# Head mean squares from two rounded products, logarithm and exponential from one activation table, gates from the hyperbolic tangent

## The chip, the core and the metric

The kernel runs on one core of a Trainium2 chip. Its time is the device time of one launch in microseconds (us), from the first to the last instruction of the program and what the launch adds around them. Times of kernels are medians of several launches; everything else is read from one profiled execution.

The core has engines that each work through a list of instructions of their own, in order, and meet only through semaphores: PE (TensorE, matrix products; its output goes to PSUM), DVE (VectorE), ACT (ScalarE, activation functions out of tables), POOL (GpSimd, here used only to start DMAs) and SP (SyncE, used only to start DMAs).

## The reference

One layer of a decoder is computed for 1024 prompt tokens and 32 sample tokens (8 sequences of 4), so for T = 1056 columns. What matters for the change:

```python
z = rms_norm(x) @ w_in       # q (12 heads of 64) | k | v | ua | ub | ga | gb
q = rms_norm(q, q_norm_w)    # over each head's 64 values
k = rms_norm(k, k_norm_w)
u = ua * sigmoid(ub)
# three groups of 4 heads: dilated window attention, merged by their denominators
a  = o_att @ w_att
cb = silu(layer_norm(causal_dwconv(u))) @ w_conv_out
h  = sigmoid(ga) * a + sigmoid(gb) * cb
x  = x + h @ w_out
x  = x + (silu(g) * up) @ w_down
```

All inputs are float32. The head norm needs, for each head and token, the mean of 64 squares; with channels on partitions that is a product with a 128 by 128 matrix which holds 1/64 where row and column belong to one head.

## The kernel before, in words

Activations lie with channels on the 128 partitions and tokens in the free dimension, cut into NCH = 3 chunks of CH = 352 columns. A weight tile of 128 output channels is a job: its 8 input blocks of 128 channels times 3 chunks. Every large product is computed in three passes of a rounded format (fp32r): weights and activations are each split in a rounded part and the remainder (`whi`, `wlo`, `xhi`, `xlo`), and hi times hi, hi times lo and lo times hi are added up in PSUM (lines 675 to 677). So one chunk of a job is 24 matmuls. ACT makes the rounded weights `whi` (lines 1134, 1197), DVE the remainder `wlo` (line 1422), two jobs ahead.

The order of all work is written out by hand. The stages are:

1. GLU jobs (16), with a loop over 8 pairs. DVE multiplies value and sigmoid and then does 13 taps of the depthwise convolution per pair (lines 1465, 1466).
2. q, k, v jobs: 3 groups of 6 jobs, two each for q, k and v. In a job i of q or k (i < 4), ACT squares each chunk into `sqb` (line 1191). While PE is in the next job, it multiplies after each chunk the squares of the job before with `headmean`, a plain float32 product (line 763, function `mean_squares`). ACT takes the logarithm (line 1186) and the exponential with factor -0.5 (line 1188), which gives the reciprocal root in `rsb`. DVE then multiplies the product in PSUM with the norm's weight and `rsb` into `zt` (line 1517, `qkv_out`) or copies v (line 1519), and does 1, 2 and 2 taps of the convolution after the three chunks; every third job it also does the convolution of the sample tokens (lines 1498 to 1502).
3. The gate stage: 48 slots q, in each of which PE does one chunk of a gate job (`dense`), ACT the sigmoid of it (`gate`, line 1210), and around that one block of the window attention proceeds in steps: scores on PE (line 860), mask and maximum on DVE (line 1558), exponentials on ACT (line 1240), turning on PE (line 876), copies on DVE and ACT, and the product with the values on PE (line 889). The first slots also hold the rest of the convolution's taps, slots 25 to 28 the LayerNorm with its logarithms and exponentials (lines 1271, 1273), and slots 31 on the products of cached keys on DVE (line 1588), each of which needs a DMA of queries (`qb`) that POOL starts when the product two before it is done. Slots 41 to 44 hold swish (`ln_act`, line 1278).
4. 24 slots of the convolution's output projection, which start when DVE has made the first remainder `slo` (line 1667, `conv_lo`). DVE multiplies with the stored gate (`conv_gate`, line 1663).
5. The att stage: 24 units of 6 matmuls each. DVE multiplies the product in PSUM with the gate (line 1739), adds the convolution branch (line 1741), ACT rounds the sum to `hhi` (line 1359) and DVE makes the remainder `hlo` (line 1748). Then w_out and the norm.
6. The feed-forward part with the other weights, from 1097 us to the end.

The gates are stored to DRAM by SP as they are made and loaded again for stages 4 and 5.

The tables of ACT hold one set of functions at a time; the build puts an `ACT_TABLE_LOAD` wherever a function needs another set.

## Time and profile before

| | |
|---|---|
| time before, median of 3 runs | 1867.81 us (1867.55 to 1868.34) |
| the profiled execution's own time | 1867.85 us |
| its span, first to last instruction | 1866.0 us |
| busy: PE, DVE, ACT, POOL | 1784.8, 1028.7, 623.3, 69.8 us |
| instructions of PE, DVE, ACT | 10441, 1443, 1029 |
| mean granted clock of PE | 0.971 |

Busy time is the time in which an engine has at least one instruction under way. A timeline row has the start and the duration in us, the engine, the line and the operation, output and inputs, how many neighbouring instructions it merges, and in brackets how long the engine was idle before it and who ended that. PE's matmuls overlap: their starts, not their durations, tell how fast they follow each other. A row of a view by line has the count, the busy time, the mean duration in ns, and the idle time before the group with what ended it.

### The profile page before, as it was taken

The page shows a single profiled execution, that of the slowest core. Times are in us where ns is not written, and L with a number is a line of the kernel's source. Part 1 is how long each engine was busy: PE and PEld are TensorE (multiplying, and loading weights), DVE is VectorE, ACT ScalarE, POOL GpSimd, SP SyncE. Part 2 cuts the span into 40 slices and gives each one's busy share as a digit, 9 for nine tenths or more (in the row PEclk, how much of TensorE's full clock was granted, in tenths as well). Part 3 has the DMA queues.
Part 4 walks back from the last instruction along what each step waited for, and adds up shares of the span by engine and source line. Part 5 has one row for each costly group of instructions (what it writes and reads, how often), then busy time and mean ns, then how long its engine had stood idle before and what let it go on. Part 6 is the DMA issues. An engine that isn't in the chain of part 4 may idle for free.

```text
span 1866.0 us, 25465 instructions
## 1 busy us (share of the span) xinstructions
PE 1784.8 (96%) x10441; PEld 1670.0 (89%) x10441; DVE 1028.7 (55%) x1443; ACT 623.3 (33%) x1029; POOL 69.8 (4%) x125
## 2 busy tenths in 40 slices
PE   5999989999999997779999999999999999999999
PEld 5899989999888887779998889899899899899897
DVE  5688988788987355673175432424424424424425
ACT  5111165957666566810032232121121121121120
POOL 0000000000000001212000000000000000000000
PEclk8999999999999998988699999999999999999999
DMA  6111333234242326975382002222222222222232
GB/s 190 57 56 56 112 102 115 91 114 150 91 145 85 138 86 191 332 261 165 103 288 91 1 34 91 91 91 91 91 91 91 91 91 90 92 90 90 92 109 103
DMA packets 156487, 211.55 MB, mean 113 GB/s; under 512 B 9090, under 2 KB 127010, under 8 KB 155603
## 3 DMA queue, kind: packets, MB, share of 16 engines
q1 hardware_dynamic: 145971, 134.01, 23.4%
q0 software_dynamic: 10416, 76.16, 10.9%
q8 instruction: 68, 1.11, 0.2%
q14 instruction: 32, 0.26, 0.0%
HBM read 180.04 MB, written 74.80 MB: 137 GB/s over the span
## 4 chain that ended last, share of the span: by engine, by line
PE 85%; DVE 5%; DMA 3%; ACT 2%; SPq 2%; DVEq 2%; issue 1%; ACTq 0%
PE ps L675 19%; PE ps L676 19%; PE ps L677 19%; PE ps L1110 4%; PE ps L1108 4%; PE ps L1109 4%; DVE conv L1466 2%; PE ps L942 2%; PE ps L1038 2%; PE ps L1040 2%; PE ps L1039 2%; DMA qb<-scr_q 1%; PE ps L889 1%; DMA raw<-w_in 1%; SPq L471 1%
## 5 line engine op out<-in xcount | busy, mean ns | idle before, releaser
L675 PE MATMUL ps<-xhi,whi 128*128 128x352 f32 x1200 | 405.4, 338 | 8.6 <-DVEq L1521 7.0
L677 PE MATMUL ps<-xhi,wlo 128*128 128x352 f32 x1200 | 388.4, 324 | 0.0
L676 PE MATMUL ps<-xlo,whi 128*128 128x352 f32 x1200 | 387.9, 323 | 0.0
L675 PE MATMUL ps<-nhi,whi 128*128 128x352 f32 x1056 | 341.7, 324 | 0.0
L676 PE MATMUL ps<-nlo,whi 128*128 128x352 f32 x1056 | 339.4, 321 | 0.0
L677 PE MATMUL ps<-nhi,wlo 128*128 128x352 f32 x1056 | 338.9, 321 | 0.0
L1466 DVE SCALAR_TENSOR_TENSOR conv<-u,vec,conv 128x1024 f32<-128x1024 f32 x240 | 308.4, 1285 | 25.6 <-issue 11.1
L1422 DVE TENSOR_TENSOR wlo<-raw,whi 128x1024 fp32r<-128x1024 f32 x126 | 153.6, 1220 | 262.0 <-ACT whi L1197 253.6
L675 PEld LDWEIGHTS ps<-xhi,whi 128*128 128x128 f32 x1200 | 228.2, 190 | 19.1 <-DVEq L1521 7.6
L676 PEld LDWEIGHTS ps<-xlo,whi 128*128 128x128 f32 x1200 | 228.5, 190 | 4.1
L677 PEld LDWEIGHTS ps<-xhi,wlo 128*128 128x128 f32 x1200 | 227.9, 190 | 0.0
L675 PEld LDWEIGHTS ps<-nhi,whi 128*128 128x128 f32 x1056 | 198.9, 188 | 1.1
L676 PEld LDWEIGHTS ps<-nlo,whi 128*128 128x128 f32 x1056 | 199.1, 189 | 0.4
L677 PEld LDWEIGHTS ps<-nhi,wlo 128*128 128x128 f32 x1056 | 198.6, 188 | 0.0
L1197 ACT CAST whi<-raw 128x1024 fp32r<-128x1024 f32 x90 | 93.9, 1044 | 277.3 <-PE ps L1103 209.2
L1829 DVE TENSOR_TENSOR x<-x,ps 128x512 f32<-128x512 f32 x176 | 118.2, 686 | 78.8 <-PE ps L1110 78.4
L1110 PE MATMUL ps<-whi,aclo 128*128 128x512 f32 x352 | 138.8, 394 | 0.0
L1108 PE MATMUL ps<-whi,achi 128*128 128x512 f32 x352 | 138.8, 394 | 0.0
L1109 PE MATMUL ps<-wlo,achi 128*128 128x512 f32 x352 | 138.2, 393 | 0.0
L1816 DVE TENSOR_TENSOR sil<-ps,sil 128x352 f32<-128x352 f32 x66 | 34.6, 525 | 124.3 <-PE ps L677 124.3
L1398 ACT ACTIVATE sil<-ps 128x352 f32<-128x352 f32 x66 | 30.7, 465 | 190.4 <-PE ps L677 190.4
L675 PE MATMUL ps<-shi,whi 128*128 128x352 f32 x192 | 69.1, 360 | 22.7 <-DVE slo L1667 21.8
(208 smaller groups left out, 2262.6 us busy)
## 6 DMA issues: line engine op xcount, KB each, us to landing
kv_sample<-cache_kv_w POOLq DMA_DIRECT2D x32, 1022.0 KB, 6.2
raw<-w_in SPq DMA_DIRECT2D x50, 512.0 KB, 4.7
raw<-w_gate_up SPq DMA_DIRECT2D x44, 512.0 KB, 3.9
scr_z<-zt SPq DMA_DIRECT2D x34, 528.0 KB, 3.2
kc<-cache_kv_w POOLq DMA_DIRECT2D x32, 512.0 KB, 6.1
qb<-scr_q POOLq DMA_DIRECT2D x24, 512.0 KB, 6.3
raw<-w_down SPq DMA_DIRECT2D x22, 512.0 KB, 4.1
kv_sample<-cache_kv_w POOLq DMA_DIRECT2D x8, 1016.0 KB, 6.6
```

What stands on the lines that cost most here:

```text
L675: pe_mm(out, wh, rhs_hi, start=first, stop=False)
L676: pe_mm(out, wh, rhs_lo, start=False, stop=False)
L677: return pe_mm(out, wl, rhs_hi, start=False, stop=last)
L942: mm = nc.tensor.matmul(ps[:, 3, hp * P + col:hp * P + col + w], kc[m % 3][:, s if g else DEC_S - 1, hp * P:(hp + 1) * P], ptr[:, g, 0, co ...
L1038: nc.tensor.matmul(dst, hhi[:, k, tok], wohi[half][:, k, :], start=k == 0, stop=False)
L1108: nc.tensor.matmul(dst, achi[i % 2][:, k, tok], whi[half][:, cc], start=k == 0, stop=False)
L1109: nc.tensor.matmul(dst, achi[i % 2][:, k, tok], wlo[half][:, cc], start=False, stop=False)
L1110: mm = nc.tensor.matmul(dst, aclo[i % 2][:, k, tok], whi[half][:, cc], start=False, stop=k == 1)
L1197: act.copy(whi[n % 2][:, :], raw[n % 2][:, :]).then_inc(s_hi, 1)
L1422: V.tensor_tensor(wlo[slot][:, :], raw[slot][:, :], whi[slot][:, :].bitcast(F32), ALU.subtract).then_inc(s_lo, 1)
L1466: return V.scalar_tensor_tensor(dst, src, w, dst, ALU.mult, ALU.add)
L1829: last = V.tensor_tensor(x1_half(t, half), x1_half(t, half), ps[0:n, d % RING, :], ALU.add)
```

## The change

The change has three parts.

- **Mean squares.** ACT squares each chunk of q and k twice, once into `sqb` in float32 and once into a rounded tile `sqh`; DVE subtracts the two into a rounded remainder `sql` (new function `square_lo`), as its first work in each chunk's step; PE multiplies both with a rounded copy `headmean_r` (made once by DVE) and adds them up in PSUM. PE now waits for `sql`.
- **Tables.** ACT loads ahead of the q, k, v jobs a set of tables that holds both logarithm and exponential.
- **Gates.** The stored gate is tanh(z/2) in place of sigmoid(z) = (1 + tanh(z/2))/2. The "+ 1" goes into the multiplications with the gates (`conv_gate`, `att_gate`), which become operations with two arithmetic steps, and the factor 0.5 into the rounding of the sum (`att_hi`, `att_lo`).

```diff
--- before.py
+++ after.py
@@ -184,6 +184,10 @@
     pb = reg("pb", [P, NH, 2 * P])
     kvv = reg("kvv", [P, KT, GW])
     assert cur2[0] <= nc.sbuf_usable_end
+    sqh = at("sqh", [P, T], F32R, U0 + KT * ULEN * 4 + 2048)
+    sql = at("sql", [P, T], F32R, U0 + KT * ULEN * 4 + 2048 + T * 4)
+    headmean_r = at("headmean_r", [P, P], F32R, U0 + KT * ULEN * 4 + 2048 + 2 * T * 4)
+    assert KT * HIST * 4 + KT * NS * 4 <= 2048 and U0 + KT * ULEN * 4 + 2048 + 2 * T * 4 + 4 * P <= nc.sbuf_usable_end
     rowqk = at("rowqk", [P, NG, 2, HD], F32, U0 + KT * ULEN * 4 + 3 * GW * 4)
     cur2 = [cur2[0] - KT * GW * 4]
     prow = reg("prow", [P, NG, 2 * P])
@@ -239,7 +243,7 @@
     s_g, s_gfd, s_a, s_af = (sem(n) for n in ("s_g", "s_gfd", "s_a", "s_af"))
     s_ufree = sem("s_ufree")
     s_sig, s_conv = sem("s_sig"), sem("s_conv")
-    s_sq, s_ssr, s_msr, s_sqrt = sem("s_sq"), sem("s_ssr"), sem("s_msr"), sem("s_sqrt")
+    s_hm, s_sq, s_sql, s_ssr, s_msr, s_sqrt = sem("s_hm"), sem("s_sq"), sem("s_sql"), sem("s_ssr"), sem("s_msr"), sem("s_sqrt")
     s_ztd, s_zta = sem("s_ztd"), sem("s_zta")
     s_zst = [sem(f"s_zst{i}") for i in range(2)]
     s_utail, s_pexp0 = sem("s_utail"), sem("s_pexp0")
@@ -752,15 +756,16 @@
         with pe.Fori(0, NG) as g:
             for i in range(6):
                 if i == 0:
-                    pe.wait_ge(s_mats, 16 * 5)
+                    pe.wait_ge(s_hm, 1)
 
                 def mean_squares(c, i=i):
                     q = NCH * (i - 1) + c
-                    pe.wait_ge(s_sq, 12 * g + (q + 1))
+                    pe.wait_ge(s_sql, 12 * g + (q + 1))
                     if q >= 2:
 
                         pe.wait_ge(s_msr, 12 * g + (q - 1))
-                    nc.tensor.matmul(ps[:, 6 + q % 2, 0:CH], headmean[:, :], sqb[:, cols(c)], start=True, stop=True).then_inc(s_ssr, 1)
+                    nc.tensor.matmul(ps[:, 6 + q % 2, 0:CH], headmean_r[:, :], sqh[:, cols(c)], start=True, stop=False)
+                    nc.tensor.matmul(ps[:, 6 + q % 2, 0:CH], headmean_r[:, :], sql[:, cols(c)], start=False, stop=True).then_inc(s_ssr, 1)
                 tile_job(i % 2, 6 * g + (QKV0 + i), xhi, xlo, (s_zfd, 3 * NCH * g + (NCH * (QKV0 // 2 + i // 2 - 1) + 1)),
                          after=mean_squares if 1 <= i <= 4 else None)
 
@@ -1172,6 +1177,7 @@
         with act.Fori(1, KT) as j:
             glu_sigmoid(j)
 
+        act.preload_act_table_set("natural_log_exp_and_others")
         for g in range(NG):
             for i in range(6):
                 m = QKV0 + 6 * g + i
@@ -1188,7 +1194,8 @@
                         act.activation(rsb[:, cols(c)], rsb[:, cols(c)], ACT.Exp, scale=-0.5).then_inc(s_sqrt, 1)
                     act.wait_ge(s_z[s], NCH * (m // 2) + c + 1)
                     if i < 4:
-                        act.activation(sqb[:, cols(c)], z(s, c), ACT.Square).then_inc(s_sq, 1)
+                        act.activation(sqb[:, cols(c)], z(s, c), ACT.Square)
+                        act.activation(sqh[:, cols(c)], z(s, c), ACT.Square).then_inc(s_sq, 1)
                 split_hi(s, m + 2, m // 2 + 1)
 
         def split_at(n):
@@ -1207,7 +1214,7 @@
             m = GATE0 + jj
             act.wait_ge(s_g, q + 1)
             act.wait_ge(s_zst[m % 2], 16 * ((m - QKV0) // 2))
-            act.activation(zt[m % 2][:, cols(c)], z(0, c), ACT.Sigmoid).then_inc(s_zta, 1)
+            act.activation(zt[m % 2][:, cols(c)], z(0, c), ACT.Tanh, scale=0.5).then_inc(s_zta, 1)
 
         def move_out(eng, g, i, sem_):
             eng.wait_ge(s_kvt, MOVE_BASE[g] + i + 1)
@@ -1356,10 +1363,10 @@
             act.wait_ge(s_ht, i + 1)
             src = sga[i // KT % 2][:, i % KT, :]
             if i < 2 * KT:
-                act.copy(hhi[:, i % KT, cols(i // KT)], src).then_inc(s_hhi, 1)
+                act.activation(hhi[:, i % KT, cols(i // KT)], src, ACT.Copy, scale=0.5).then_inc(s_hhi, 1)
             else:
-                act.copy(hhi[:, i % KT, 2 * CH:SEQ], src[:, 0:PC2])
-                act.copy(hl[:, i % KT, 0:NS], src[:, PC2:CH]).then_inc(s_hhi, 1)
+                act.activation(hhi[:, i % KT, 2 * CH:SEQ], src[:, 0:PC2], ACT.Copy, scale=0.5)
+                act.activation(hl[:, i % KT, 0:NS], src[:, PC2:CH], ACT.Copy, scale=0.5).then_inc(s_hhi, 1)
 
         for i in range(NCH * KT):
             att_hi(i)
@@ -1503,6 +1510,7 @@
 
         dve.wait_ge(s_qkw, 16 * 4)
         dve.wait_ge(s_mats, 16 * 5)
+        V.tensor_copy(headmean_r[:, :], headmean[:, :]).then_inc(s_hm, 1)
         def qkv_out(m, c):
 
             g, i, s = (m - QKV0) // 6, (m - QKV0) % 6, m % 2
@@ -1521,10 +1529,16 @@
             dve.drain().then_inc(s_zfd[s], 1)
 
 
+        def square_lo(g, i, c):
+            dve.wait_ge(s_sq, 12 * g + NCH * i + c + 1)
+            V.tensor_tensor(sql[:, cols(c)], sqb[:, cols(c)], sqh[:, cols(c)].bitcast(F32), ALU.subtract).then_inc(s_sql, 1)
+
         for g in range(NG):
             for i in range(6):
                 m = QKV0 + 6 * g + i
                 for c in range(NCH):
+                    if i < 4:
+                        square_lo(g, i, c)
                     if m > QKV0:
                         qkv_out(m - 1, c)
                     v0 = KT * TAPS_GLU + TAPS_QKV * (m - QKV0)
@@ -1660,7 +1674,7 @@
             j, c = (q - CO_SLOT) // NCH, q % NCH
             dve.wait_ge(s_sgc[j % 2], 16 * (j // 2 + 1))
             dve.wait_ge(s_g, q + 1)
-            V.tensor_tensor(ha[:, j, cols(c)], z(0, c), sgc[j % 2][:, cols(c)], ALU.mult).then_inc(s_gfd, 1)
+            V.scalar_tensor_tensor(ha[:, j, cols(c)], sgc[j % 2][:, cols(c)], 1.0, z(0, c), ALU.add, ALU.mult).then_inc(s_gfd, 1)
 
         def conv_lo(k):
             dve.wait_ge(s_shi, k + 1)
@@ -1736,7 +1750,7 @@
                 dve.wait_ge(s_sga[c], 16)
             dve.wait_ge(s_a, i + 1)
             r = UNITS.index(("att", i))
-            V.tensor_tensor(g, ps[:, r % RING, 0:CH], g, ALU.mult).then_inc(s_af, 1)
+            V.scalar_tensor_tensor(g, g, 1.0, ps[:, r % RING, 0:CH], ALU.add, ALU.mult).then_inc(s_af, 1)
             dve.drain()
             V.tensor_tensor(g, g, ha[:, j, cols(c)], ALU.add).then_inc(s_ht, 1)
 
@@ -1745,10 +1759,10 @@
             c, j = i // KT, i % KT
             dve.wait_ge(s_hhi, i + 1)
             if c < 2:
-                V.tensor_tensor(hlo[:, j, cols(c)], sga[c % 2][:, j, :], hhi[:, j, cols(c)].bitcast(F32), ALU.subtract).then_inc(s_hlo, 1)
+                V.scalar_tensor_tensor(hlo[:, j, cols(c)], sga[c % 2][:, j, :], 0.5, hhi[:, j, cols(c)].bitcast(F32), ALU.mult, ALU.subtract).then_inc(s_hlo, 1)
             else:
-                V.tensor_tensor(hlo[:, j, 2 * CH:SEQ], sga[c % 2][:, j, 0:PC2], hhi[:, j, 2 * CH:SEQ].bitcast(F32), ALU.subtract)
-                V.tensor_tensor(hl[:, j, NS:2 * NS], sga[c % 2][:, j, PC2:CH], hl[:, j, 0:NS].bitcast(F32), ALU.subtract).then_inc(s_hlo, 1)
+                V.scalar_tensor_tensor(hlo[:, j, 2 * CH:SEQ], sga[c % 2][:, j, 0:PC2], 0.5, hhi[:, j, 2 * CH:SEQ].bitcast(F32), ALU.mult, ALU.subtract)
+                V.scalar_tensor_tensor(hl[:, j, NS:2 * NS], sga[c % 2][:, j, PC2:CH], 0.5, hl[:, j, 0:NS].bitcast(F32), ALU.mult, ALU.subtract).then_inc(s_hlo, 1)
 
         def residual(half, t):
             n, o = rows_of(t), NT * half + t
```

The line numbers of the changed kernel are higher by 4 to 14.

How the instructions stand on the engines shows at three places. First ACT in slots 3 to 6 of the gate stage. `zt` is the gate's output, `pb` the probabilities of an attention block, `ob` and `pt` its outputs and turned probabilities. Before:

```order
L1197 CAST whi_62<-raw_60 128x1024
L1240 ACT_TABLE_LOAD
L1240 ACTIVATE pb,ob_90<-pb,nmx 128x128 x4
L1210 ACT_TABLE_LOAD
L1210 ACTIVATE zt_70<-ps 128x352
L1252 COPY pt<-ps 128x256
L1240 ACT_TABLE_LOAD
L1240 ACTIVATE pb,ob_91<-pb,nmx 128x256 x4
L1210 ACT_TABLE_LOAD
L1210 ACTIVATE zt_70<-ps 128x352
```

With the change:

```order
L1204 CAST whi_62<-raw_60 128x1024
L1247 ACTIVATE pb,ob_90<-pb,nmx 128x128 x4
L1217 ACTIVATE zt_70<-ps 128x352
L1259 COPY pt<-ps 128x256
L1247 ACTIVATE pb,ob_91<-pb,nmx 128x256 x4
L1217 ACTIVATE zt_70<-ps 128x352
```

The loads between gates and exponentials are gone. In the whole program ACT's table loads fall from 144 to 15; six of the 15 stand in the LayerNorm, where each logarithm and each exponential still has one.

Second DVE, from the end of the GLU stage's taps to the first head norm of the q, k, v jobs. Before:

```order
L1489 COPY utail<-u 128x256
L1466 SCALAR_TENSOR_TENSOR conv<-u,vec,conv 128x1024 x5
L1498 TENSOR_TENSOR sprod<-u,vec 128x992
L1500 TENSOR_REDUCE conv<-sprod 128x32
L1502 TENSOR_SCALAR conv<-conv,vec 128x32
L1422 TENSOR_TENSOR wlo_64<-raw_60,whi_62 128x1024
L1517 SCALAR_TENSOR_TENSOR zt_69<-ps,qkw,rsb 128x352
```

With the change:

```order
L1496 COPY utail<-u 128x256
L1513 CAST headmean_r<-headmean 128x128
L1534 TENSOR_TENSOR sql<-sqb,sqh 128x352
L1473 SCALAR_TENSOR_TENSOR conv<-u,vec,conv 128x1024
L1534 TENSOR_TENSOR sql<-sqb,sqh 128x352
L1473 SCALAR_TENSOR_TENSOR conv<-u,vec,conv 128x1024 x2
L1534 TENSOR_TENSOR sql<-sqb,sqh 128x352
L1473 SCALAR_TENSOR_TENSOR conv<-u,vec,conv 128x1024 x2
L1505 TENSOR_TENSOR sprod<-u,vec 128x992
L1507 TENSOR_REDUCE conv<-sprod 128x32
L1509 TENSOR_SCALAR conv<-conv,vec 128x32
L1429 TENSOR_TENSOR wlo_64<-raw_60,whi_62 128x1024
```

After the last row there come a fourth `sql` and then the first `zt`. One rounding and four subtractions now stand ahead of that first `zt`, which PE waits for.

Third PE, after the first chunk of the second q job. Before:

```order
L677 MATMUL ps<-xhi,wlo_65 128x352
L763 MATMUL ps<-sqb,headmean 128x352
L675 MATMUL ps<-xhi,whi_63 128x352
L676 MATMUL ps<-xlo,whi_63 128x352
L677 MATMUL ps<-xhi,wlo_65 128x352
```

With the change:

```order
L767 MATMUL ps<-sqh,headmean_r 128x352
L768 MATMUL ps<-sql,headmean_r 128x352
L679 MATMUL ps<-xhi,whi_63 128x352
L680 MATMUL ps<-xlo,whi_63 128x352
L681 MATMUL ps<-xhi,wlo_65 128x352
```

One plain float32 product has become two rounded ones; there are 36 such places.

## Rows read from the trace of the kernel before

**Rows 1.** the page, part 1: busy us, share of the span, instructions

```profile
PE 1784.8 (96%) x10441; PEld 1670.0 (89%) x10441; DVE 1028.7 (55%) x1443; ACT 623.3 (33%) x1029; POOL 69.8 (4%) x125
```

**Rows 2.** by stretch: ends, length, PE, PEld, DVE, ACT, POOL, clock, DMA, GB/s

```profile
300.00:390.00 90.00, 90.00 (x546) 87.45 (x546) 74.70 (x78) 57.25 (x71) 0.97 (x2) 1.00 0.36 110
...
471.00:544.00 73.00, 70.18 (x502) 65.59 (x502) 66.46 (x123) 52.08 (x112) 0.00 (x0) 1.00 0.26 84
...
690.00:726.00 36.00, 26.36 (x187) 24.67 (x187) 17.12 (x50) 21.60 (x52) 4.28 (x8) 0.87 0.60 175
...
765.00:805.00 40.00, 18.19 (x114) 17.93 (x113) 25.68 (x22) 28.86 (x30) 11.61 (x18) 0.79 1.06 366
```

**Rows 3.** timeline of PE, us: start, duration, line, operation

```profile
323.69 0.33 PE L677 MATMUL ps<-xhi,wlo 128*128 128x352 f32 x1
323.85 0.75 PE L763 MATMUL ps<-sqb,headmean 128*128 128x352 f32 x2
...
328.26 0.76 PE L763 MATMUL ps<-sqb,headmean 128*128 128x352 f32 x2
```

**Rows 4.** timeline of PE, then DVE: PE waits for DVE's backlog

```profile
239.00 0.75 PE L763 MATMUL ps<-sqb,headmean 128*128 128x352 f32 x2
...
255.62 0.66 PE L675 MATMUL ps<-xhi,whi 128*128 128x352 f32 x1 [7.02 <-DVEq L1521]
...
244.32 6.72 DVE L1466 SCALAR_TENSOR_TENSOR conv<-u,vec,conv 128x1024 f32<-128x1024 f32 x5
...
254.94 0.58 DVE L1517 SCALAR_TENSOR_TENSOR zt<-ps,qkw,rsb 128x352 f32<-128x352 f32 x1
```

**Rows 5.** waits of line 1517, whole and from 327.5; then DVE's timeline

```profile
  ACT rsb L1188: 24.1, 26
...
  ACT rsb L1188: 15.5, 19
...
327.53 0.84 DVE L1517 SCALAR_TENSOR_TENSOR zt<-ps,qkw,rsb 128x352 f32<-128x352 f32 x1
...
470.89 1.29 DVE L1466 SCALAR_TENSOR_TENSOR conv<-u,vec,conv 128x1024 f32<-128x1024 f32 x1 [0.19 <-issue]
```

**Rows 6.** timelines of DVE, then PE, in the att stage

```profile
961.03 0.52 DVE L1748 TENSOR_TENSOR hlo<-sga,hhi 128x352 fp32r<-128x352 f32 x1
961.47 0.52 DVE L1739 TENSOR_TENSOR sga<-ps,sga 128x352 f32<-128x352 f32 x1
...
973.95 0.50 PE L1038 MATMUL ps<-wohi,hhi 128*128 128x512 f32 x1 [0.26 <-DVE sga L1739]
```

**Rows 7.** groups of ACT by line; then who waited for line 1240

```profile
L1210 ACT ACT_TABLE_LOAD x32 | 41.1, 1283 | 5.3 <-DMA scr_z<-zt 4.7
...
L1240 ACT ACT_TABLE_LOAD x24 | 30.8, 1283 | 0.4
...
L1191 ACT ACTIVATE sqb<-ps 128x352 f32<-128x352 f32 x36 | 16.3, 452 | 27.8 <-PE ps L677 27.8
...
  PE ps L876: 15.4, 4
```

**Rows 8.** timeline of PE, two neighbouring slots of the gate stage

```profile
501.39 1.78 PE L889 MATMUL ps<-kvv,pt 128*128 128x64 f32 x15
...
509.08 1.89 PE L889 MATMUL ps<-kvv,pt 128*128 128x64 f32 x16
```

**Rows 9.** timelines of ACT, DVE and PE at the gate stage's end

```profile
764.20 1.28 ACT L1210 ACT_TABLE_LOAD   x1
765.50 0.46 ACT L1210 ACTIVATE zt<-ps 128x352 f32<-128x352 f32 x1
...
766.93 1.23 DVE L1422 TENSOR_TENSOR wlo<-raw,whi 128x1024 fp32r<-128x1024 f32 x1 [5.35 <-ACT whi L1197]
...
776.16 1.23 DVE L1588 TENSOR_TENSOR kc<-kc,qb 128x1024 f32<-128x1024 f32 x1 [3.11 <-DMA qb<-scr_q]
...
804.81 0.63 PE L675 MATMUL ps<-shi,whi 128*128 128x352 f32 x1 [21.81 <-DVE slo L1667]
```

## The prediction

> **What bounds the kernel now.** I read the page first, then the stretches, then the timelines of single stages. The page [rows 1] shows PE busy for 1784.8 of 1866.0 us and DVE for 1028.7. So a saving on another engine counts only where PE waits for that engine, and the question for each part of the change is which wait ends last in its stage. The stretches [rows 2] separate the stages: in the q, k, v jobs (300 to 390 us) PE is busy all the time and DVE 83%; in the gate stage (471 to 544) PE is busy 70.2 of 73 and DVE 66.5; from 690 to 726 PE is busy only 26.4 of 36, and from 765 to 805 only 18.2 of 40. The feed-forward part behind 1097 us has nothing that the change touches.
>
> In the q, k, v jobs the pitch from one mean-square product to the next is 328.26 - 323.85 = 4.41 us, the same as PE's own work; PE waits nowhere for ACT, although ACT reloads its tables twice a chunk. The one pause is at the start: DVE comes out of the GLU stage with taps still to do, reaches the head norm of the first job at 254.94, and PE waits 7.02 us for the bank it frees [rows 3, 4]. DVE waits here for `rsb`, 24.1 us in 26 waits, 15.5 of them behind 327.5 us [rows 5].
>
> In the gate stage two products with the values that follow each other are 509.08 - 501.39 = 7.69 us apart, and that is PE's own work of a slot without a gap [rows 8].
>
> **The sum, against 1867.85 us, the profiled execution's own time** (0.04 us above the median of the runs shown).
>
> *Mean squares on PE.* A rounded pass takes 323.85 - 323.69 = 0.16 us. A chunk's 24 passes take 3.82, so the float32 product takes 4.41 - 3.82 = 0.59 us [rows 3]. Two rounded passes take 0.32. That is 0.27 us less, 36 times 9.7 us. But PE can have this only where it isn't made to wait, and DVE is close behind.
>
> *Mean squares on DVE.* 36 subtractions of 128x352 are added. No row shows this one, the nearest does the same operation on the same size, `hlo` = `sga` - `hhi`, which takes 961.47 - 961.03 = 0.44 us from start to start [rows 6]. The bounds: 0.44, and 0.76, which is what the head norm takes with a wait and a drain (0.58 us, and some 0.18 before the next row of its kind starts [rows 4, 5]). I take 0.44, since the new operation has no drain behind it. With 0.2 us for rounding `headmean` DVE gets 16.0 us more.
>
> *Does DVE then set the pace?* Walk through the stage from 244.32, where DVE starts it. Four subtractions and the rounding lie ahead of the first `zt`: DVE frees the bank 2.0 us later, PE resumes at 257.6. A part of PE's pause moves forward: PE now waits for the first `sql` from 239.00, where the first product of this kind stands [rows 4], to 244.9 us, and then again; both end with DVE. In group 0 PE then saves 9 products times 0.27 = 2.4 us, so at the head of group 1 it is where it was, and so is DVE: by then it has done 16 of the subtractions and has lost most of its 8.6 us of waits. I put that point at 327.5 as before [rows 5]. From there to 470.89, where the last v copy is done, DVE needed 143.4 us, of which 15.5 were waits, so 127.9 of work. The 20 subtractions left make it 136.7 us. PE in the same two groups needs less: its last pass would end 24 x 0.27 = 6.5 us earlier, and the v jobs and the copies behind it follow. So both give about the same end: DVE 327.5 + 136.7 = 464.2, plus some 0.5 of waits left, 464.7. **The stage ends 6.2 us earlier.** The bounds: 8.1 us, if all 24.1 us of waits vanish against 16.0 of work; and nothing, if each subtraction costs 0.76 (36 x 0.32 = 11.5 us more, of which PE's slack takes a part).
>
> *Squares on ACT.* 36 more of 0.45 us, 16 us, and 72 loads less of 1.283 us [rows 7], 92 us. ACT gets lighter and hides both; of its time only the waits of DVE counted, which are in the walk.
>
> *Loads in the gate stage.* 32 ahead of gates and 24 ahead of exponentials go, 72 us of ACT's time [rows 7]. None of it is on the path in the slots, where PE follows itself [rows 8]. PE waited for exponentials 15.4 us in four places, but in each ACT had its table loaded and was waiting for DVE's maxima. The 10 us of pause between 690 and 726 [rows 2] come from SP, which has 41 stores of keys and values to issue before the one that frees an output buffer: unchanged. Slots 41 to 47 are different. There DVE's products of cached keys wait for their queries (3.11 us at 776.16 [rows 9]), each DMA starts only when an earlier product is done, and the first remainder, which ends PE's pause of 21.81 us at 804.81, stands behind the last product of slot 47. Into this chain goes one wait for ACT, 5.35 us at 766.93: the weights' rounding there stands behind swish and one reloaded gate table at 764.20. Swish still needs its own load, the gate's goes. So 1.3 us come off. The load takes 1.28 us and the gate starts 1.30 behind its start [rows 9].
>
> The Trainium skill, "ScalarE: Activation LUTs", section "What ACT_TABLE_LOAD costs", says that every switch costs a load of about 1283 ns and a drain of about 1380 ns, 2.66 us in all. The first figure agrees with the trace, the second doesn't show there; by the page's figure this term would be 2.7 and the time 1860.3.
>
> *Operations with two steps.* `att_gate`, `att_lo` and `conv_gate` get an operation like `zt`'s, 0.58 us where the present one has 0.52 [rows 4, 6]. In the att stage DVE is the bound: three operations a unit, 1.49 us, and PE waits for them at 973.95 [rows 6]. Ten units pass until then, each with two longer operations: 10 x 2 x 0.06 = 1.2 us more. Behind that PE leads. `conv_gate` waits for PE, 0.1 us. The rounding on ACT has slack of about 0.4 us a unit. Together + 1.3 us. The bounds are 0 and 3.
>
> Sum: -6.2 - 1.3 + 1.3 = -6.2 from 1867.85, **1861.7 us**.
>
> **The rivals.**
>
> *The gain is used up before it arrives (same time).* Either two rounded passes take as long as one float32 product did (the pitch stays 4.41), or a subtraction costs 0.6 us or more. In the first case PE's end of the stage moves from 460 to 462 and no wait goes: 1867.9. In the second DVE gets 22 us instead of 16 against the 24.1 us of waits: 1867 or so. For it speaks how little DVE has spare; against it the rows of the same operation.
>
> *Slower.* DVE takes its subtraction first in each step, and everything behind it (head norm, taps, weights' remainder) stands behind a new wait for ACT's second square. The place is groups 1 and 2, where a head norm costs 0.3 us more than in group 0 (0.84 against 0.58 [rows 4, 5]) and DVE has the longest tiles. If each subtraction costs 0.76 with its wait, DVE gets 27.6 us for 24.1, and the 2.0 us at the start are 3.2: the stage ends about 5 us later, 1873. It decides from 0.67 us a subtraction on, where 36 of them equal the waits. Against it speaks that ACT is rid of 2.57 us of loads a chunk and its squares come earlier than `rsb` did.
>
> *ACT was the bound after all (more gain).* If the loads stood in the way of the exponentials which PE waited for, four waits would shorten by 1.28 each: 5.1 us more, 1856.6. The skill's page named above, section "Table sets: the hidden batching unit", makes grouping of functions by set a rule, which would promise this. The trace speaks against it: the idle time of the exponentials follows the load and ends with the maxima.
>
> **How the numbers follow.** The forecast gets 0.55, the used-up gain 0.25, slower 0.09, more gain 0.11. A change of 0.2% (3.7 us) is about what the measurement can tell from none. Around the forecast lie 1858.5 to 1864. The range of 8 in 10 reaches from 1857 into the cases with no change: 1857 to 1867.5. Faster by over 0.2%: 0.55 + 0.11 less a little of the forecast's own upper edge, 0.64; within: 0.27; slower: 0.09.
>
> **What would show it.** The pitch of the mean squares is 4.14 us at the start of groups 1 and 2. PE waits for `sql` from about 239 to 245 and again until 257.6. The waits of DVE for `rsb` are all but gone, replaced by less than 5 us for the squares. The last v copy ends near 464.7. Slots stay at 7.69 us. The first `slo` product starts 7.5 us earlier than 804.81, near 797.3; the feed-forward part's length is unchanged. Wrong would be the forecast if the subtraction shows over 0.6 us, if PE's pitch stays above 4.3, or if slots get shorter.

## The result, and the profile after

The changed kernel takes 1873.49 us (median of 9 executions, 1867.64 to 1878.01), the kernel before on the same chip 1868.75 (median of 9): 1.0024 times as long, 95% interval 1.0013 to 1.0035. The prediction of 1861.7 us and its range (1857 to 1867.5) were wrong: the change costs 4.7 us. The profiled execution took 1874.7 us with a span of 1872.9, against 1867.85 and 1866.0 before.

Much of what the prediction said of single rows came true, and one row that it did not have undid it. This is PE's only row with a wait between 224 and 262 us in the changed kernel; in brackets stand the idle time ahead of the instruction and what ended it:

```profile
245.31 0.66 PE L679 MATMUL ps<-xhi,whi 128*128 128x352 f32 x1 [20.67 <-DVE headmean_r L1513]
```

It is the first product of the q, k, v jobs. PE has done the GLU stage's last pass at 224.6 and stands for 20.67 us before it starts the first q job. The pause of 7.02 us at the second job [rows 4] is gone. DVE's timeline shows what PE waited for:

```profile
237.83 6.72 DVE L1473 SCALAR_TENSOR_TENSOR conv<-u,vec,conv 128x1024 f32<-128x1024 f32 x5
244.47 0.28 DVE L1495 COPY ptail<-u 128x240 f32<-128x240 f32 x1
244.66 0.28 DVE L1496 COPY utail<-u 128x256 f32<-128x256 f32 x1
244.86 0.22 DVE L1513 CAST headmean_r<-headmean 128x128 fp32r<-128x128 f32 x1
252.62 0.53 DVE L1534 TENSOR_TENSOR sql<-sqb,sqh 128x352 fp32r<-128x352 f32 x1 [7.54 <-ACT sqh L1198]
```

The copy of `headmean` takes 0.22 us, but it stands behind the last taps of the GLU stage. It ends at 245.1 and PE starts 0.2 us later. Then DVE, which was behind, has nothing to do for 7.54 us, because PE has only now begun the job whose squares it needs. The backlog of one engine has become idle time of both.

The page and the stretches of the changed kernel (columns as in [rows 1] and [rows 2]):

```profile
PE 1778.1 (95%) x10441; PEld 1670.5 (89%) x10441; DVE 1042.9 (56%) x1480; ACT 471.8 (25%) x936; POOL 69.8 (4%) x125
```

```profile
224.00:257.00 33.00, 12.33 (x63) 12.04 (x63) 21.48 (x24) 4.32 (x7) 2.30 (x5) 0.69 0.47 166
300.00:390.00 90.00, 90.00 (x566) 90.00 (x565) 82.75 (x92) 31.32 (x61) 0.97 (x2) 1.00 0.38 118
477.00:550.00 73.00, 70.19 (x501) 65.60 (x500) 66.88 (x123) 31.92 (x96) 0.00 (x0) 1.00 0.26 86
```

ACT has lost 152 us, DVE has gained 14, PE has lost 7 us of work. PE does 566 instructions in the 90 us in which it did 546 [rows 2]; the gate stage's stretch reads as it did, although ACT has 20 us less in it. And in the first stretch PE has only 12.33 of 33 us, at a granted clock of 0.69.

PE's rows of the mean squares in group 1, which answer to [rows 3]:

```profile
335.77 0.32 PE L767 MATMUL ps<-sqh,headmean_r 128*128 128x352 f32 x1
335.93 0.32 PE L768 MATMUL ps<-sql,headmean_r 128*128 128x352 f32 x1
...
339.91 0.32 PE L767 MATMUL ps<-sqh,headmean_r 128*128 128x352 f32 x1
...
344.04 0.32 PE L767 MATMUL ps<-sqh,headmean_r 128*128 128x352 f32 x1
```

The pitch is 4.14 and 4.13 us, from 4.41. In the groups of DVE the waits for `rsb` (24.1 us [rows 5]) are gone from the head norm, and the remainder's are 13.6 us, half of which is the row of 7.54 above (columns: line, engine, operation, shapes, count; busy us, mean ns; idle us ahead of them, and its releaser):

```profile
L1525 DVE SCALAR_TENSOR_TENSOR zt<-ps,qkw,rsb 128x352 f32<-128x352 f32 (+2 forms) x44 | 27.4, 653 | 0.0
L1534 DVE TENSOR_TENSOR sql<-sqb,sqh 128x352 fp32r<-128x352 f32 x36 | 18.7, 521 | 13.8 <-ACT sqh L1198 13.6
```

The balance of the q, k, v stage: 20.67 us of pause for 7.02 is 13.65 more. After the pause PE runs at the lower of its two clocks (1.2 GHz, a granted clock of 0.50) for a while, and the first pass is 0.66 us long instead of 0.32. These are the stretch behind the pause, the last pass of the first chunk, and the first and last pass of the second chunk:

```profile
245.30:250.10 4.80, 4.79 (x16) 4.80 (x17) 0.00 (x0) 0.00 (x0) 0.00 (x0) 0.50 0.00 0
```

```profile
251.40 0.32 PE L681 MATMUL ps<-xhi,wlo 128*128 128x352 f32 x1
251.56 0.32 PE L679 MATMUL ps<-xhi,whi 128*128 128x352 f32 x1
...
255.22 0.32 PE L681 MATMUL ps<-xhi,wlo 128*128 128x352 f32 x1
```

From the first to the last of 24 passes the first chunk takes 251.40 - 245.31 = 6.09 us and the second 3.66, so the clock costs 2.4 us. The kernel before pays for its shorter pause too: the 24 passes behind the 7.02 us take 260.96 - 255.62 = 5.34 us, which is 1.7 more than 3.66.

```profile
260.96 0.32 PE L677 MATMUL ps<-xhi,wlo 128*128 128x352 f32 x1
```

So the clock costs 0.7 us more than before, and the mean squares give back 36 x 0.27 = 9.7. Together 4.7 us more. Measured from ACT's last sigmoid of the GLU stage (223.94 before, 224.67 now) to the first v move, PE's first turning of v (470.85 and 476.6), the stage takes 251.9 us against 246.9 before: 5.0 more.

### The profile page after: what moved, and what is told of

The parts are those of the page before. It is cut to its first block, busy times and chain, and to the rows that moved or that the text cites. A ratio compares the mean times of both kernels' runs of the same rounds, so it can differ in the third digit from the quotient of the medians.

```text
span 1872.9 us, 25409 instructions
## 1 busy us (share of the span) xinstructions
PE 1778.1 (95%) x10441; PEld 1670.5 (89%) x10441; DVE 1042.9 (56%) x1480; ACT 471.8 (25%) x936; POOL 69.8 (4%) x125
## 4 chain that ended last, share of the span: by engine, by line
PE 82%; DVE 7%; DVEq 3%; DMA 3%; SPq 1%; issue 1%; ACT 1%; ACTq 0%
PE ps L679 19%; PE ps L680 18%; PE ps L681 18%; PE ps L1115 4%; PE ps L1113 4%; PE ps L1114 4%; DVE conv L1473 3%; DVEq L1529 2%; PE ps L947 2%; PE ps L1043 2%; PE ps L1045 2%; PE ps L1044 2%; DMA qb<-scr_q 1%; PE ps L894 1%; SPq L475 1%
## 5 line engine op out<-in xcount | busy, mean ns | idle before, releaser
L679 PE MATMUL ps<-xhi,whi 128*128 128x352 f32 x1200 | 395.5, 330 | 22.2 <-DVE headmean_r L1513 20.7
L1429 DVE TENSOR_TENSOR wlo<-raw,whi 128x1024 fp32r<-128x1024 f32 x126 | 153.5, 1220 | 255.3 <-ACT whi L1204 246.9
L1204 ACT CAST whi<-raw 128x1024 fp32r<-128x1024 f32 x90 | 93.9, 1044 | 276.7 <-PE ps L1108 209.2
L1113 PEld LDWEIGHTS ps<-whi,achi 128*128 128x128 f32 x352 | 66.1, 188 | 15.6
```

What stands on the lines that cost most here:

```text
L679: pe_mm(out, wh, rhs_hi, start=first, stop=False)
L1113: nc.tensor.matmul(dst, achi[i % 2][:, k, tok], whi[half][:, cc], start=k == 0, stop=False)
L1204: act.copy(whi[n % 2][:, :], raw[n % 2][:, :]).then_inc(s_hi, 1)
L1429: V.tensor_tensor(wlo[slot][:, :], raw[slot][:, :], whi[slot][:, :].bitcast(F32), ALU.subtract).then_inc(s_lo, 1)
```

## The experiments

Two theories stood after this. **Theory 1**: the parts do what the prediction said, and the place of one wait costs more than they bring. **Rival**: the squares are worth little or nothing (DVE gives back what PE gains, or ACT does), and the loss is theirs. Each ratio is to the kernel before on the same chip, with its 95% interval.

### The copy made early, and the wait alone

`e1_early` is the changed kernel with the copy moved ahead of the taps of the second GLU pair:

```diff
             if j == 0:
                 conv_params()
+            if j == 1:
+                dve.wait_ge(s_mats, 16 * 5)
+                V.tensor_copy(headmean_r[:, :], headmean[:, :]).then_inc(s_hm, 1)
...
-        V.tensor_copy(headmean_r[:, :], headmean[:, :]).then_inc(s_hm, 1)
```

> The changed kernel, with one line of DVE moved: the rounded copy of headmean is made in the second pair of the GLU stage and no longer behind all of its taps. PE's wait for it stays where it is, ahead of the first q job. Theory 1 (the position of that wait alone cost the gain): PE's pause of 20.67 us ahead of the first q job goes, a pause of some 6 us comes at the first mean square (for the remainder) and one of 3 to 4 us ahead of the third job; the third job starts at about 257.7 us where it is some 271 now, the first move of v starts 7 us earlier than before's 470.85, and the time is 6 to 8 us below the kernel before (ratio 0.996 to 0.997). Theory 2 (DVE has no room for the 36 subtractions): the pause is gone but the last v copy ends at 470 us or later all the same, ratio 0.999 to 1.001.

`e2_wait` is the kernel before with nothing of the change but the late copy and the wait for it (the plain product stays):

```diff
-                    pe.wait_ge(s_mats, 16 * 5)
+                    pe.wait_ge(s_hm, 1)
...
         dve.wait_ge(s_mats, 16 * 5)
+        V.tensor_copy(headmean_r[:, :], headmean[:, :]).then_inc(s_hm, 1)
```

> The kernel before with nothing of the change but the wait: DVE makes the rounded copy of headmean behind the GLU taps (nobody reads it), and PE waits for it ahead of the first q job. Theory 1: PE pauses some 20.7 us at 224.6, the old pause of 7.02 at 255.62 goes with it, all else shifts; PE has 13 to 16 us more to wait than before and nothing to win it back with, so the time is 1880 to 1884 (ratio 1.007 to 1.0085). Theory 2 (the pause is covered, since PE waited there for DVE's taps anyway, and the changed kernel lost its time elsewhere): ratio 1.000 to 1.002.

`e1_early` took 1861.38 us, ratio 0.9964 (0.9952 to 0.9977); `e2_wait` 1882.86, ratio 1.0075 (1.0062 to 1.0088). So the wait alone costs 14.4 us, and taking it out of the changed kernel gives 12.1 back. PE's rows with a wait at this place, of `e1_early` first, then of `e2_wait`:

```profile
243.57 0.66 PE L767 MATMUL ps<-sqh,headmean_r 128*128 128x352 f32 x1 [5.55 <-DVE sql L1536]
256.25 0.43 PE L679 MATMUL ps<-xhi,whi 128*128 128x352 f32 x1 [1.79 <-DVEq L1531]
```

```profile
243.98 0.66 PE L677 MATMUL ps<-xhi,whi 128*128 128x352 f32 x1 [20.68 <-DVE headmean_r L1508]
```

The two pauses of `e1_early` are the ones that the prediction described: until about 244.9 for the first remainder and until 257.6 for the bank (this execution's first square is 1.2 us earlier than before's). The expectation had put the second at 3 to 4 us, and it is 1.79. In `e2_wait` the wait stands ahead of the first job's products, although none of them reads the copy.

### The wait at its first use

In `e1b_use` the copy stays late; only PE's wait moves down to where its value is first needed:

```diff
-                if i == 0:
-                    pe.wait_ge(s_hm, 1)
...
+                    if q == 0:
+                        pe.wait_ge(s_hm, 1)
                     pe.wait_ge(s_sql, 12 * g + (q + 1))
```

> The changed kernel with one line moved: PE asks for the rounded headmean ahead of its first product with it, and no longer ahead of the first q job. The copy itself stays where the change put it, behind the last tap of the GLU stage. Theory 1 (the place of the wait costs the gain): the pause of 20.67 us ahead of the first q job is gone; the copy ends 0.3 us ahead of the first remainder, which PE has to wait for anyhow, until about 245; so the time is that of the kernel with the early copy, 1861.4, within 2 us. Rival (the late copy itself costs, since it stands ahead of the first remainder on DVE): 0.2 us more, which can't be seen. Rival (the early copy gained by something else, the layout of the GLU stage): the time stays near 1873. The remainder's own first wait, about 5.5 us ahead of the first product of this kind, should stand in the trace, as the prediction had it.

It took 1860.93 us, ratio 0.9959 (0.9943 to 0.9975), the same as with the early copy. Its first pause is the remainder's:

```profile
246.19 0.66 PE L766 MATMUL ps<-sqh,headmean_r 128*128 128x352 f32 x1 [5.69 <-DVE sql L1533]
```

So the late copy costs nothing that can be seen. What cost was that the wait for it stood one job ahead of its use. Theory 1 holds; the rest asks what each part brings once this is mended.

### The tables: gates alone, preloaded set alone, both

`e3_gates` is the kernel before with the gates' part (tanh, `Copy` with scale 0.5, the two-step operations); `e4_table` has the one line `act.preload_act_table_set("natural_log_exp_and_others")` ahead of the q, k, v jobs; `t34` has both.

```diff
-            act.activation(zt[m % 2][:, cols(c)], z(0, c), ACT.Sigmoid).then_inc(s_zta, 1)
+            act.activation(zt[m % 2][:, cols(c)], z(0, c), ACT.Tanh, scale=0.5).then_inc(s_zta, 1)
...
-            V.tensor_tensor(g, ps[:, r % RING, 0:CH], g, ALU.mult).then_inc(s_af, 1)
+            V.scalar_tensor_tensor(g, g, 1.0, ps[:, r % RING, 0:CH], ALU.add, ALU.mult).then_inc(s_af, 1)
```

> The kernel before with the gates' part alone: tanh for the stored gates, the +1 and the 0.5 in the later operations; mean squares and their tables as before. The forecast's terms: 1.3 us less at the end of the gate stage (one reloaded table in the chain of the cached keys) and up to 1.3 us more in the att stage, where the after-trace showed 42.6 us between the turned outputs and the first w_out product as before, so nearer to nothing. Theory 1: ratio 0.999 to 1.000. Theory 2 (table loads between gates and exponentials stood in PE's way): 5 us or more less, ratio under 0.9975, and slots shorter than 7.69 us.

> The kernel before with the preloaded set alone: logarithm and exponential need no load in the q, k, v jobs (72 loads, 92 us of ACT, less); products, squares and gates as before. Theory 1 (PE paces the stage and does not wait for ACT): the pitch of the mean squares stays 4.41 us and DVE only waits less for rsb; the first move of v starts 0 to 3 us earlier, ratio 0.9985 to 1.000. Theory 2 (ACT was close behind PE and paced it): pitch under 4.41 us or the move over 5 us earlier, ratio under 0.997.

> The kernel before with the gates by tanh and the preloaded set, and without the squares' part: what the change gives by its tables alone. Theory 1: ACT is off the path in the q, k, v jobs and in the slots, so only the chain of cached keys gains, 1.3 to 1.5 us, on top of what the preloaded set alone gave (4.0, of which the start of the q, k, v jobs had 1.1 us by the run's own beginning): 1863 to 1867. Pitch stays 4.41, the pause of 7 us ahead of the second q job stays. Rival (the tables are the gain): at or below 1862.

The three took 1868.60 (ratio 0.9999, 0.9988 to 1.0010), 1864.47 (0.9980, 0.9969 to 0.9992) and 1866.21 us (0.9989, 0.9978 to 1.0000). `e4_table` lies just under the range that its expectation gave (0.9985 to 1.000); its pitch stays 4.41 and the v move comes 2 us earlier, so neither sign of its theory 2 is there. By the medians the set brings 4 us alone and 2 with the gates, and little of it in the q, k, v jobs: from the first square to the first v move these stages take 243.1, 242.3 and 242.4 us, before 243.0. In the trace of `e4_table` 1.1 us of the 3.9 lie ahead of these jobs, where the two kernels are the same; no run shows how much of the rest is the set's. The waits of the head norm for `rsb` stay at 22.2 us in `t34`, because there the mean product on PE comes only every 4.41 us, whatever ACT does.

### The squares alone

`e5_squares` is the changed kernel with the early copy, without the preloaded set and with the gates of before.

> The kernel before with the squares' part alone: rounded square, remainder, two products, copy of headmean made early; sigmoid gates and both table sets stay. Theory 1 (PE sets the pace in the q, k, v jobs and the squares relieve it): pitch 4.14 instead of 4.41, the first v move 8 us earlier than 470.85, the time 5 to 8 us under the kernel before, 1860.5 to 1863.5; the reloads stay hidden (ACT has 57 of 90 us busy before, and gets 20 x 0.45 more). Rival (the reloads stand in the way once two squares are in ACT's chain): PE waits for the remainder in many chunks, the remainder waits for ACT's second square over 5 us in all, and the time is no better than 1866. Rival (the gain of the kernel with the early copy is that of the tables): 1868.

It took 1870.62 us, ratio 1.0014 (1.0003 to 1.0024). **The forecast of theory 1 failed**: the squares alone bring nothing, and the expectation's first rival, the reloads in ACT's way, describes what happened. The kernel's waits in the q, k, v stage (waiting engine and line, releaser; us in total, times, longest), and ACT's timeline over one of its turns (from one logarithm to the next):

```profile
PE ps L679 <- DVEq L1530: 9.8, 4, 3.2
DVE sql L1535 <- ACT sqh L1197: 9.7, 13, 1.9
```

```profile
328.11 0.56 ACT L1191 ACTIVATE rsb<-ps,eps 128x352 f32<-128x352 f32 x1
328.73 1.28 ACT L1193 ACT_TABLE_LOAD   x1
330.02 0.50 ACT L1193 ACTIVATE rsb<-rsb 128x352 f32<-128x352 f32 x1
330.43 0.45 ACT L1196 ACTIVATE sqb<-ps 128x352 f32<-128x352 f32 x1
330.77 0.46 ACT L1197 ACTIVATE sqh<-ps 128x352 fp32r<-128x352 f32 x1
331.24 1.28 ACT L1191 ACT_TABLE_LOAD   x1
332.54 0.55 ACT L1191 ACTIVATE rsb<-ps,eps 128x352 f32<-128x352 f32 x1
```

ACT works without a gap here, and one turn takes 332.54 - 328.11 = 4.43 us. PE's is 4.14. With its two reloads ACT is slower than PE, DVE waits for ACT's second square, PE for DVE's banks, and the stage takes 245.0 us instead of 243.0. In the kernel before, ACT's turn without a gap is 342.57 - 338.49 = 4.08 us, 0.34 shorter, and PE's was 4.41:

```profile
333.48 0.56 ACT L1186 ACTIVATE rsb<-ps,eps 128x352 f32<-128x352 f32 x1 [0.36 <-PE ps L763]
...
338.49 0.56 ACT L1186 ACTIVATE rsb<-ps,eps 128x352 f32<-128x352 f32 x1
...
342.57 0.56 ACT L1186 ACTIVATE rsb<-ps,eps 128x352 f32<-128x352 f32 x1
```

Even these 0.3 us were not spare. Once a job ACT also rounds weights, and that turn takes 338.49 - 333.48 = 5.01 us. Over the three chunks of a job ACT needs 4.08 + 4.08 + 5.01 = 13.2 us, and PE 3 x 4.41 = 13.2: the reloads were just hidden. With two squares and the reloads it is 4.43 + 4.43 + 5.36 (332.54 to 337.90) = 14.2 us against 12.4. In the changed kernel, without reloads, ACT waits for PE in each of these turns, mostly 2.3 us:

```profile
340.43 0.56 ACT L1192 ACTIVATE rsb<-ps,eps 128x352 f32<-128x352 f32 x1 [2.29 <-PE ps L768]
341.06 0.50 ACT L1194 ACTIVATE rsb<-rsb 128x352 f32<-128x352 f32 x1
341.47 0.45 ACT L1197 ACTIVATE sqb<-ps 128x352 f32<-128x352 f32 x1
341.81 0.46 ACT L1198 ACTIVATE sqh<-ps 128x352 fp32r<-128x352 f32 x1
```

The Trainium skill, "ScalarE: Activation LUTs", section "Table sets: the hidden batching unit", wants functions grouped by set. The runs give that rule a condition: in this stage grouping is worth under 1 us while PE is not the faster one, and it decides over the squares' whole gain as soon as another part makes PE faster than ACT with its reloads.

### Squares and set, without the gates

The test of that (theory 2) is `e8_sqtab`: `e1_early` with sigmoid gates and one-step operations.

> The changed kernel with the early copy and without its gates' part: squares and the preloaded set, sigmoid gates. Theory 2 (new, from the kernel with the squares alone, 1870.6: with two reloads and two squares ACT's own turn of a chunk is 4.43 us, above PE's 4.14, so ACT takes the place of PE as the bound and only the set lets the squares pay): pitch 4.14, PE waits for DVE only at the start of the jobs, first v move near 462, time 1861 to 1864, the gates' part being worth 0 to 1.5 us. Rival (the parts add up: squares +2, set -4): 1866 to 1867. Rival (the gates by tanh are needed too): 1866 or above.

It took 1863.48 us, ratio 0.9970 (0.9957 to 0.9983): two parts that bring 0.14% of loss and 0.20% of gain alone bring 0.30% of gain together, which is just beyond what the three intervals leave open. The first square to the first v move takes 234.8 us, and PE waits for DVE only at the start, 5.6 and 1.9 us. Against the set alone (0.9980) the intervals of the whole time overlap; the stage shows what the squares add to it, 242.3 us there and 234.8 here. In whole time it shows between `t34` and `e1_early`, 0.9989 and 0.9964, which differ by the squares' part. What `e1_early` has beyond `e8_sqtab` is the gates' part, and the intervals of the two overlap.

### How much room DVE has

`e6_double` is `e1_early` with each remainder computed twice, first into a place that nobody reads:

```diff
+            V.tensor_tensor(sqj[:, 0:CH], sqb[:, cols(c)], sqh[:, cols(c)].bitcast(F32), ALU.subtract)
             V.tensor_tensor(sql[:, cols(c)], sqb[:, cols(c)], sqh[:, cols(c)].bitcast(F32), ALU.subtract).then_inc(s_sql, 1)
```

> The changed kernel with the early copy and each remainder computed twice, first into a place that nobody reads: 36 x 0.44 = 15.9 us more on DVE in the q, k, v jobs. It prices the prediction's rival that each subtraction costs 0.76 or more. Theory 1 (with the change PE and DVE are about even: DVE waits for nothing after the first remainder but has gaps of 0.18 us, PE waits 7.3 us at the start alone): most of it shows, PE waits for banks in groups 1 and 2, pitch above 4.4 there, first v move 10 to 16 us later than 461.3, time 1870 to 1877. Rival (DVE still has room, 7 of 90 us not busy): under half of it shows, 1868 or less.

It took 1873.30 us, ratio 1.0019 (1.0009 to 1.0029), 11.9 us above `e1_early`, for 15.9 us of work. The stage takes 248.5 us instead of 234.7. PE waits for banks seven times, once at the start (3.1 us) and six times behind it, 6.6 us together:

```profile
PE ps L681 <- DVEq L1533: 9.7, 7, 3.1
```

All six stand ahead of a job; within the jobs the pitch stays near 4.14 us, where the expectation had it above 4.4. DVE and PE are indeed about even after the change. Had a subtraction cost twice its 0.44 us, the change would have been a loss even with the wait at its place.

### Fewer taps in the GLU stage

The idea was that what is left at the start of the q, k, v jobs is a backlog of DVE from the whole GLU stage. `e7_taps` is `e1_early` with 12 taps for each pair in the GLU stage instead of 13; `e7_taps11` has 11; `e9_sqtab12` has 12 and sigmoid gates. The taps taken out are done in the gate stage's slots.

```diff
-TAPS_GLU = 13
+TAPS_GLU = 12
```

> The changed kernel with the early copy and 12 instead of 13 taps for each channel block in the GLU stage; the 8 taps taken out (8 x 1.28 = 10.3 us of DVE) are done in the gate stage's slots, where the taps then take 21 slots instead of 18. A version that could beat both. Theory 1 (after the early copy what is left at the start of the q, k, v jobs is DVE's arrears from the GLU stage: 5.55 us ahead of the first mean product and 1.79 ahead of the next bank): both pauses go, the first v move stands 4 to 7 us earlier, at 455 to 457, and the gate stage keeps its length, since the slots are set by PE: 1855 to 1858. Rival (DVE is as full in the slots, 66.5 of 73 us busy, as it was in the GLU stage): the taps there end late, slots get longer or the first product of the layer norm waits for the last tap, and the time is 1861 or above.

> As the kernel with 12 taps, with 11: another 10.3 us of DVE moved from the GLU stage to the slots, where the taps then take 24 of 48. The kernel with 12 gave 1855.4; its pauses at the start of the q, k, v jobs are 4.2 and 1.3 us, and its gate stage was shorter (exponentials were waited for 3.4 us instead of 6.0). Theory (arrears of DVE are what is left): the two pauses fall under 3 us together and the time is 1851 to 1854. Rival (what is left of the pause is the latency from bank over square and remainder to the product, no arrears): 1855 to 1856. Rival (the slots are full): 1857 or above, the layer norm's first product waits for a tap.

> Squares and preloaded set with the early copy and 12 taps in the GLU stage, sigmoid gates: the kernel with 12 taps without its gates' part. Theory (the gates' part is worth its one load in the chain of cached keys, 1.3 to 1.5 us, and nothing else): 1856 to 1858, against 1855.4 with it. Rival (its two-step operations cost about what it gains): 1854.5 to 1856.

They took 1855.38 (ratio 0.9923, 0.9907 to 0.9938), 1852.20 (0.9914, 0.9902 to 0.9927) and 1855.21 us (0.9932, 0.9920 to 0.9944). `e7_taps11` beats both kernels, by 0.9% and more; the intervals of the three overlap, so no order among them is shown. The first two times were as expected. The third was not: it lies in the range of its rival, so with 12 taps, too, the gates' part is worth nothing that can be seen. The reason given for the first two failed in the q, k, v jobs. PE's pauses at the start in `e7_taps`, then in `e7_taps11`:

```profile
243.03 0.66 PE L767 MATMUL ps<-sqh,headmean_r 128*128 128x352 f32 x1 [4.20 <-DVE sql L1536]
255.71 0.43 PE L679 MATMUL ps<-xhi,whi 128*128 128x352 f32 x1 [1.27 <-DVEq L1531]
```

```profile
242.32 0.66 PE L767 MATMUL ps<-sqh,headmean_r 128*128 128x352 f32 x1 [3.30 <-DVE sql L1536]
254.99 0.43 PE L679 MATMUL ps<-xhi,whi 128*128 128x352 f32 x1 [2.46 <-DVEq L1531]
```

They fell from 7.3 to 5.5 us with 12 taps and no further with 11 (5.8, where under 3 was expected), and the stage from 234.7 to 233.6 and 234.0, not by the 4 to 7 expected. DVE's waits in the GLU stage (60 to 226 us) tell why; these are `e1_early`, `e7_taps` and `e7_taps11`:

```profile
DVE u L1482 <- ACT sg L1173: 10.0, 8, 3.2
```

```profile
DVE u L1482 <- ACT sg L1173: 18.9, 8, 3.2
```

```profile
DVE u L1482 <- ACT sg L1173: 30.1, 15, 3.3
```

With 13 taps already, DVE has done a pair's taps and waits for the next pair's sigmoids, so nothing adds up from pair to pair. What stands ahead of the first remainder is the last pair's own taps (13 of some 1.35 us), which can start only when that pair's products are done. Of the eight taps taken out only this pair's one shortens the pause, by 1.35 us (5.55 to 4.20); the others became waiting of DVE. The time from the first remainder to the first head norm, behind which the second pause ends, is 12.57 us in all three.

The larger piece is in the gate stage, which takes 160.3 us from the first v move to the first product of the layer norm, 159.6 with 11 taps, and 164.1 in `e1b_use`. In all three kernels with fewer taps it takes 159.6 to 161.3 us, in the other eleven traces of this case 162.8 to 167.5; PE's waits for the exponentials are 3.2 to 3.4 us in it, and 4.3 to 6.0 in the other eleven. In `e1b_use` stands a pause ahead of group 2's first probabilities, and DVE's rows ahead of the maxima for them are these (PE, then DVE):

```profile
588.76 1.45 PE L880 MATMUL ps<-ident,pb 128*128 128x128 f32 x6 [2.31 <-ACT pb L1246]
```

```profile
580.31 1.19 DVE L1504 TENSOR_TENSOR sprod<-u,vec 128x992 f32<-128x992 f32 x1
581.58 1.19 DVE L1506 TENSOR_REDUCE conv<-sprod 128x32 f32<-128x992 f32 x1
582.85 0.24 DVE L1508 TENSOR_SCALAR conv<-conv,vec 128x32 f32<-128x32 f32 x1
583.42 1.23 DVE L1428 TENSOR_TENSOR wlo<-raw,whi 128x1024 fp32r<-128x1024 f32 x1 [0.33 <-issue]
```

A block's last tap brings about 3 us of further work for the sampled positions, and with 13 taps it fell into the one slot whose maxima PE waits for. With 12 it falls elsewhere: between the taps and the weights' remainder nothing stands, and the pause is gone. In `e7_taps` (DVE's timeline):

```profile
573.44 4.01 DVE L1473 SCALAR_TENSOR_TENSOR conv<-u,vec,conv 128x1024 f32<-128x1024 f32 x3
577.37 1.22 DVE L1429 TENSOR_TENSOR wlo<-raw,whi 128x1024 fp32r<-128x1024 f32 x1
578.50 0.42 DVE L1585 COPY pt<-ps 128x256 f32<-128x256 f32 x1
```

That accounts for 2.3 of the 3.8 us by which the gate stage is shorter in these two traces. No run was made for the rest, and none moves the last tap alone, so this part is read from the traces and not shown by an experiment.

## Why the prediction was wrong

**The step that failed** is the one on PE's pause: "PE now waits for the first `sql` from 239.00 [...] to 244.9 us, and then again". It took the pause to begin at the first product with the remainder. But the change also replaced PE's wait for the mats, which stands ahead of the first q job, by one for the rounded copy, and that copy stands on DVE behind every tap of the GLU stage. The prediction counted the copy's 0.2 us as work of DVE and never asked who waits for it, from where. It had DVE's number, 244.32 [rows 4], as the start of its own walk; that PE is ready for the first job 20 us earlier it didn't look up. With this step right the sum is the prediction's own 1861.7 + 20.7 less the two pauses of 5.5 and 1.8 us that it replaces (as `e1_early` has them), about 1875; measured were 1873.5. `e1b_use`, with 1860.9 us, shows that nothing else of this size was missing. None of the three signs that the prediction named for being wrong appeared (a subtraction over 0.6 us, a pitch over 4.3, shorter slots): they watched the rivals, not this wait.

**The pause and the walk of the two engines**, as described, came true in `e1_early` and `e1b_use`, in both places.

**Mean squares on PE** (9.7 us less): right, 4.14 us a turn. **On DVE** (36 x 0.44): right, `sql` starts 0.44 us ahead of the `zt` behind it, and takes 0.52 in all.

**The stage's end, 6.2 us earlier**: with the wait at its place the stage got 8.3 us shorter in `e1_early` and 8.2 in `e1b_use`. That is the bound of 8.1, not the value taken: the head norm's waits of 24.1 us vanish altogether, and 1.2 us for the second square take their place. The walk had the head of group 1 where it was, and there it went wrong: counted from the first square it comes 2.2 us earlier in `e1_early` (93.9 us instead of 96.1 to that group's first mean product). From there on the stage gains 6.2 us, as the walk said. That the forecast of the total came so near to `e1b_use` is in part luck: the stage gave 2 us more than its term and the two-step operations cost nothing, and the time shows 1.2 us of these 3.3 (7.4 less than before instead of 6.2), which is no more than such medians can tell.

**The gate stage's slots**: right. Line 894, which answers to [rows 8], starts at 507.04 and 514.75 in the changed kernel, 7.71 us apart. PE waits 16.2 us in four places for the exponentials, 15.4 before [rows 7], with 24 loads less; the longest, the pause between 690 and 726, was 9.6 us before and is 10.2.

**The chain of cached keys, 1.3 us less**: from the first product of cached keys to the first `slo` it takes 108.1 us instead of 109.6 in the changed kernel, 1.5 less, and 108.3 in `e3_gates`. All eight traces with the gates' part have 108.1 to 109.2, the six without it 108.9 to 110.7 (means 108.6 and 109.7). So some 1.1 us of gain is in the traces; in whole time the gates' part is 0 within 0.1% (`e3_gates`).

**Two-step operations, 1.3 us more**: wrong, they cost nothing. In the att stage the gate takes 514 ns on average, 518 before, the remainder 518 and 520:

```profile
L1753 DVE SCALAR_TENSOR_TENSOR sga<-sga,ps 128x352 f32<-128x352 f32 x13 | 6.7, 514 | 0.0
...
L1762 DVE SCALAR_TENSOR_TENSOR hlo<-sga,hhi 128x352 fp32r<-128x352 f32 x11 | 5.7, 518 | 0.0
```

From the joining of heads to the first output product it is 42.6 us in both kernels. The prediction took the 0.58 us of `zt`'s operation for the price of a second step; that row has two steps too, so the step isn't what makes it longer.

**The rivals.** "The gain is used up" and "slower" were both about DVE's subtraction and both did not happen; the result was on the slower side by a mechanism that no rival named. That "slower" had the stage 5 us longer and 1873 us, the very numbers measured, is luck: it reached them by subtractions of 0.76 us, and they take 0.44. "ACT was the bound after all" was judged right for the kernel before, but the prediction's sentence that ACT's lighter load "hides both" passed over something: that lighter load is the condition for the squares' gain, as the kernel with the squares alone shows.

## What to carry to other kernels

When a change replaces a wait by another, look at both ends of the new one: what stands on the releasing engine ahead of the signal, and how far ahead of its first use the waiting engine asks. An operation of 0.2 us behind a backlog, asked for one job too early, cost 12 to 14 us here. Put the wait at the first use, or the operation ahead of the backlog.

Before an edit that makes the slowest engine faster, work out the turn of each other engine in that stage, not its busy share: ACT at 57 of 90 us seemed to have room, but over a job of three chunks it needed 13.2 us, as many as PE. A gain of 0.27 us a turn on PE and a second square of 0.34 on ACT turned that round. The squares were worth nothing alone, and with the set of tables they took 7.5 us off their stage.

Before work is moved off an engine that seems to be behind, look whether it waits in the stage it is moved from: only what stands between its last wait and the signal counts.

## What was not expected of the hardware

A pause of PE cost more than its length. After 20.67 us of idling the first pass took 0.66 us instead of 0.32, and the first chunk of 24 passes 6.09 us instead of 3.66 from its first start to its last, with a granted clock of 0.50 from 245.3 to 250.1; after 7.02 us of idling the kernel before took 5.34. A pass of 0.66 us stands also behind the 5.55 us of `e1_early` and behind the 7.02 of the kernel before [rows 4].

On DVE an operation with two steps on 128x352 took 514 to 518 ns, no longer than the one-step operation in its place (518 to 520).

Executions of one kernel lay up to 10 us apart (1867.64 to 1878.01 for the changed one). Profiles of kernels with the same gates and taps differ in the gate stage by more than 4 us (`e3_gates` 167.5 us from v move to layer norm at a granted clock of 0.96, `e6_double` 162.9 at 0.98; `e1_early` 167.3, `e1b_use` 164.1), with nearly the same waits for the exponentials, so a difference of 2 us between two kernels here needs the median, not two traces.
